# One-hots of an expert scatter moved from VectorE to GpSimd and ScalarE

## The reference

```python
u = U[ib]                                   # [tokens, 8 heads, 16 picks, 2048]
h = gelu(einsum('thkd,td->thk', u, xb))
w = gate * h
y = einsum('thk,thkd->td', w, V[ib])
```

## Time and profile before

| | |
|---|---|
| median of 3 runs | 3977.99 us (3966.75 to 3984.16) |
| profiled execution | 3977.78 us |
| its span | 3975.9 us |
| mean granted TensorE clock | 0.911 |
| busy: PE, DVE, POOL, ACT | 84%, 47%, 25%, 13% |
| units 9 to 15 of the U stage | 1789.4 to 2133.1 us |
| scatter of the second half | 2133.1 to 2200.4 us |
| V stage | 2200.4 to about 2755 us |

### The profile page before, as it was taken

How to read it: one execution, slowest core, us unless ns; L and a number is a source line. 1 busy time by engine, 2 the same in 40 slices (tenths; PEclk the granted TensorE clock), 3 DMA queues, 4 the chain that set the end, 5 groups by cost and what they waited for, 6 DMA issues and landing times. The chain is left out here.

```text
span 3975.9 us, 37603 instructions
## 1 busy us (share of the span) xinstructions
PE 3338.9 (84%) x15266; PEld 2682.0 (67%) x15266; DVE 1868.3 (47%) x3292; ACT 499.1 (13%) x835; POOL 998.5 (25%) x678
## 2 busy tenths in 40 slices
PE   7999999999989946300236999997999999999999
PEld 6878887888878835200134555553888788889888
DVE  3892102100000788998999544444244545555200
ACT  1002111100002100100013000001122122222100
POOL 0000000000000347877784454443000111112000
PEclk9999999999999977655557999998999999999999
DMA  4333332344364899999994899996333222221342
GB/s 167 141 135 138 139 120 81 128 157 150 130 234 155 303 387 371 377 348 357 366 335 154 289 337 332 348 332 248 117 117 117 106 85 85 79 81 64 138 151 103
DMA packets 164645, 795.35 MB, mean 200 GB/s; under 512 B 15064, under 2 KB 64728, under 8 KB 98920
## 3 DMA queue, kind: packets, MB, share of 16 engines
q1 hardware_dynamic: 106408, 419.61, 30.1%
q0 software_dynamic: 58064, 373.33, 25.2%
HBM read 790.78 MB, written 2.10 MB: 199 GB/s over the span
## 5 line engine op out<-in xcount | busy, mean ns | idle before, releaser
L351 PE MATMUL PS<-mem,ring 128*128 128x256 f32 (+1 forms) x4608 | 1035.2, 387 | 0.0
L351 PEld LDWEIGHTS PS<-mem,ring 128*128 128x128 f32 x4608 | 880.4, 191 | 152.4 <-issue 4.6
L957 POOL DMA_INDIRECT mem<-in_peer_u,idx x256 | 566.1, 2211 | 390.9 <-DVE mem L1398 155.3
L1690 PE MATMUL PS<-mem,ring 128*128 128x256 f32 x2816 | 640.3, 383 | 9.9 <-DVE ring L2078 9.9
L1398 DVE CUSTOM_DVE_ANT_0 mem<-mem 128x2048 f32<-128x2048 f32 x256 | 584.4, 2283 | 40.8 <-DMA mem<-in_peer_u,idx 40.1
L1690 PEld LDWEIGHTS PS<-mem,ring 128*128 128x128 f32 x2816 | 530.4, 192 | 84.5 <-issue 16.3
L1421 DVE SCALAR_TENSOR_TENSOR mem<-mem 128x768 f32<-128x768 f32 x256 | 260.9, 1019 | 294.8 <-DMA mem<-in_peer_vg,idx 287.6
L1123 PE MATMUL PS<-mem 128*128 128x128 f32 x512 | 132.7, 394 | 306.9 <-DVE mem L1386 305.5
L968 POOL DMA_INDIRECT mem<-in_peer_vg,idx x256 | 282.3, 1103 | 341.3 <-DVE mem L1421 298.6
L1123 PEld LDWEIGHTS PS<-mem 128*128 128x128 f32 x512 | 99.5, 255 | 340.4 <-DVE mem L1386 262.8
L1666 POOL TENSOR_TENSOR mem<-mem,ring 128x512 f32<-128x512 f32 x84 | 111.2, 1342 | 787.2 <-DVE mem L2183 575.0
(11 more groups left out here) (338 smaller groups left out, 2810.2 us busy)
## 6 DMA issues: line engine op xcount, KB each, us to landing
ring<-in_first_tiles SPq DMA_DIRECT2D x144, 1024.0 KB
ring<-in_dn_tiles SPq DMA_DIRECT2D x88, 1024.0 KB, 4.9
mem<-in_peer_vd SPq DMA_DIRECT2D x128, 640.0 KB
ring<-in_out_panels SPq DMA_DIRECT2D x16, 2048.0 KB, 8.8
ring<-in_w_out SPq DMA_DIRECT2D x8, 2048.0 KB, 12.5
ring<-in_peer_wq SPq DMA_DIRECT2D x8, 2048.0 KB, 8.7
ring<-in_mem_w_kv SPq DMA_DIRECT2D x8, 2048.0 KB, 34.0
mem<-in_peer_u,idx POOLq DMA_INDIRECT x256, 7.5
```

The lines of the kernel that those rows point to most:

```text
L351: last = nc.tensor.matmul(PS[:, 4 + n % 4, 0:T if wide else TX], wslot[:, slot_of[n], k, :], x, start=(k == 0), stop=(k == KT - 1))
L957: nc.gpsimd.indirect_dma_start(Ug[:, at % US, :], None, a["peer_u"][0], bass.IndirectOffsetOnAxis(ap=idx[:, n, j:j + 1], axis=0)).then_inc ...
L1690: ins = nc.tensor.matmul(bank_of(n), wts[:, n % WS, k, :], hT[:, k, :], start=(k == 0), stop=(k == KT - 1))
```

## The change

The one-hots no longer come from DVE alone. In the first half POOL makes `first`, each behind a gather, and ACT makes `second` in two activations, Abs(i2 - iota) and Relu(1 - that). They are spread over units 9 to 15 (112 steps, 128 tokens). In the second half DVE makes `first`, and POOL makes `second`, behind the first four V gathers. ACT's `gates` of a unit move behind its one-hots, and `picks_evict(0)` to unit 8. PE waits for two semaphores in place of one.

```diff
-        FIRST_HOT = 12
+        FIRST_HOT = PH + 1
+        STEPS = (HN - FIRST_HOT) * PTOP
+        def hot_tokens(at):
+            s = at - FIRST_HOT * PTOP
+            return range(s * P // STEPS, (s + 1) * P // STEPS) if s >= 0 else range(0)
...
                                 bass.IndirectOffsetOnAxis(ap=idx[:, n, j:j + 1], axis=0)).then_inc(u_in[at % US], 16)
+                            for t in hot_tokens(at):
+                                pool.wait_ge(it_out, 1)
+                                if t >= OS:
+                                    pool.wait_ge(oh_used, t - OS + 1)
+                                nc.gpsimd.tensor_scalar(first[:, t % OS, :], iota[:, :], turned[:, 0, t:t + 1],
+                                                        turned[:, 2, t:t + 1], ALU.is_equal, ALU.mult).then_inc(hot_pool, 1)
...
+                            if at == GS:
+                                for t in range(P, MT * P):
+                                    pool.wait_ge(it_out, MT)
+                                    pool.wait_ge(oh_used, t - OS + 1)
+                                    nc.gpsimd.tensor_scalar(second[:, t % OS, :], iota[:, :], turned[:, 1, t - P:t - P + 1],
+                                                            None, ALU.is_equal).then_inc(hot_pool, 1)
...
-                            pe.wait_ge(oh_ready, n + 1)
+                            pe.wait_ge(hot_pool, n + 1)
+                            if m == 0:
+                                pe.wait_ge(hot_act, n + 1)
+                            else:
+                                pe.wait_ge(hot_dve, t + 1)
...
-                            act.wait_ge(oh_ready, P * m)
+                            act.wait_ge(hot_pool, P)
+                            act.wait_ge(hot_act, P)
...
+                    def second_hot(t):
+                        act.wait_ge(it_out, 1)
+                        if t >= OS:
+                            act.wait_ge(oh_used, t - OS + 1)
+                        nc.scalar.activation(second[:, t % OS, :], iota[:, :], ACT.Abs, bias=turned[:, 1, t:t + 1],
+                                             scale=-1.0).then_inc(hot_abs, 1)
+                        act.wait_ge(hot_abs, t + 1)
+                        nc.scalar.activation(second[:, t % OS, :], second[:, t % OS, :], ACT.Relu, bias=1.0,
+                                             scale=-1.0).then_inc(hot_act, 1)
...
-                        for later in beside.get(n, ()):
-                            gates(later)
-                            done += 1
...
-                        if n == FIRST_HOT - 2:
+                        if n == PH:
                             picks_evict(0)
-                        if n >= FIRST_HOT:
-                            for g in range(8 * (n - FIRST_HOT), 8 * (n - FIRST_HOT) + 8):
-                                w_evict(g)
+                        for j in range(PTOP):
+                            for t in hot_tokens(n * PTOP + j):
+                                second_hot(t)
+                                if t % 4 == 3 and t > 3:
+                                    w_evict(t // 4 - 1)
+                        for later in beside.get(n, ()):
+                            gates(later)
+                            done += 1
                         gelu(n)
...
-                    def one_hots(n):
+                    def first_hot(n):
...
-                        nc.vector.tensor_scalar(second[:, n % OS, :], iota[:, :], turned[:, 1, t:t + 1], None, ALU.is_equal)
                         nc.vector.tensor_scalar(first[:, n % OS, :], iota[:, :], turned[:, 0, t:t + 1], turned[:, 2, t:t + 1],
-                                                ALU.is_equal, ALU.mult).then_inc(oh_ready, 1)
+                                                ALU.is_equal, ALU.mult).then_inc(hot_dve, 1)
...
-                            if n >= FIRST_HOT:
-                                for t in range(2):
-                                    one_hots(2 * (at - FIRST_HOT * PTOP) + t)
```

More of the change, by code:

```diff
@@ L903, in build @@
              m_scale, m_scaled, mt_done, mt_out, h_sum, h_roots, h_scale, xn_done, q_out, sc_done, sc_out, chain, max_ready,
-             exp_ready, found, den_ready, u_used, gelu_ready, w_ready, kk_taken, kv_taken, it_done, it_out, oh_ready, oh_used, w_done,
+             exp_ready, found, den_ready, u_used, gelu_ready, w_ready, kk_taken, kv_taken, it_done, it_out, hot_pool, hot_abs, hot_act,
+             hot_dve, oh_used, w_done,
              w_out, vd_used, vg_used, y_dense, y_added, f_squares, f_roots, f_scale, y_ready, f_chain, xn2_ready, nt_done,
@@ L910, in build @@
                 "found", "den_ready", "u_used", "gelu_ready", "weights_ready", "kk_taken", "kv_taken", "picks_transposed",
-                "picks_out", "onehot_ready", "onehot_used", "scatter_done", "scatter_out", "vd_used", "vg_used", "y_dense",
+                "picks_out", "onehot_pool", "onehot_distance", "onehot_act", "onehot_dve", "onehot_used", "scatter_done",
+                "scatter_out", "vd_used", "vg_used", "y_dense",
                 "y_added", "f_squares", "f_roots", "f_scale", "y_ready", "f_chain", "xn2_ready", "xn2_transposed", "hT_out", "pool_step",
@@ L1261, in _ @@
                     picks_evict(1)
-                    for g in range(P // 4, MT * P // 4):
+                    for g in range(P // 4 - 1, MT * P // 4):
                         w_evict(g)
@@ L1382, in one_hots @@
                             dve.wait_ge(it_out, m + 1)
-                        if n >= OS:
-                            dve.wait_ge(oh_used, n - OS + 1)
-                        nc.vector.tensor_scalar(second[:, n % OS, :], iota[:, :], turned[:, 1, t:t + 1], None, ALU.is_equal)
+                        dve.wait_ge(oh_used, n - OS + 1)
                         nc.vector.tensor_scalar(first[:, n % OS, :], iota[:, :], turned[:, 0, t:t + 1], turned[:, 2, t:t + 1],
-                                                ALU.is_equal, ALU.mult).then_inc(oh_ready, 1)
+                                                ALU.is_equal, ALU.mult).then_inc(hot_dve, 1)
                     for n in range(2):
@@ L1411, in _ @@
                     for n in range(P, MT * P):
-                        one_hots(n)
+                        first_hot(n)
                     for n in range(HN):
```

## The result

The changed kernel takes 4083.76 us (median of 4 runs) against 3981.07 us for the kernel before in the same session: ratio 1.0258, 95% interval 1.0237 to 1.028. The profiled execution has a span of 4082.3 us, 106.4 us more than before.

A forecast was written before the change was run, and what follows sets the result against it. The prediction took DVE to bound heads 12 to 15, with POOL gathers let in only between products. It summed 3978 + 21 (first half) + 5 (second half) = 4004 us, with a range of 3945 to 4068.

The forecast's parts named there:

- What bounds the kernel; losses reach the end whole: Heads 9 to 15 and second-half scatter: DVE bounds heads 12 to 15; the V stage waits, so losses reach the end.
- A gather is let in only between products: POOL instructions reading SBUF enter only between two-input DVE instructions; gathers end about 0.81 us behind a product, 0.94 us free.
- I take 0.3 us: First half: assumed length of one POOL one-hot, taken from a POOL select of 0.29 us.
- So the gather waits for a whole further product: Heads 9 to 15: four-buffer loop grows from 9.96 to 12.85 us, 3.21 us a step, +21 us with late rows.
- DVE's gain, at most 40 us: Heads 12 to 15: without one-hots on DVE, steps fall from 3.12 to 2.49 us at best, 40 us gained.
- ACT costs nothing: First half: `second` as two activations makes ACT 1.7 us a step where 3.1 are there, so no cost.
- Rival 4: First half: ACT reloads its table for Abs and Relu, 1.28 us a load, over +140 us; chance 0.02.
- Second half, +5 us from 0.49 us a token: Second-half scatter: a token goes from 0.45 to 0.49 us with DVE and POOL partly overlapping, +5 us.
- My upper bound of 0.63 a token: Second half: DVE and POOL one-hots strictly in turn, 0.29 + 0.34 us a token, a loss of 23 us.
- Rival 1: First half: the gather slips in right behind the one-hot, 2.65 us a step, about 3955 us; chance 0.18.
- Rival 2: First half: half the steps slip in, some 2.93 us a step, about 3979 us, no change; chance 0.22.
- Rival 3: First half: two products lost for a gather, 3.8 us a step, +92, about 4070 us; chance 0.18.

The follow-up runs named there:

- run 7: Kernel before the change, with DVE's product replaced by a one-input sum over the same buffer: 3960.31 us, ratio 0.995.
- run 8: Changed kernel with DVE's product replaced by a one-input sum over the same buffer: 3945.52 us, ratio 0.9924.
- run 5: Changed kernel with three memsets in place of each POOL one-hot of the first half: 3980.44 us, ratio 1.0004.
- run 6: Changed kernel with POOL's first-half one-hot made over 32 of its 128 columns: 4044.48 us, ratio 1.0184.
- run 3: Changed kernel without POOL one-hots: first half `first` on DVE, `second` on ACT; second half as before the change: 3953.55 us, ratio 0.9934.
- run 4: Changed kernel with both first-half one-hots on ACT, second half as before the change: 3958.08 us, ratio 0.9947.
- run 12: Kernel with only the second half changed, its POOL one-hot made over 32 of 128 columns: 3972.42 us, ratio 0.9979.
- run 11: The kernel of run 3 measured once more, on the chip of run 10: 3955.53 us, ratio 0.9931.
- run 10: The kernel of run 3, but ACT makes `first` for every second token of the first half: 3957.58 us, ratio 0.9937.
- run 9: Changed kernel with POOL's one-hots in groups behind every fourth gather instead of behind each: 4082.87 us, ratio 1.0248.

## Why the prediction was off

The direction and the place were right: slower, in heads 9 to 15, with gathers and one-hots held to the ends of products. The size was not: +26 us forecast, 103 measured, above the range, which ended at 4068. The first half is off by 73 us (365 forecast, 437.9 measured), the second by 10.

1. *What bounds the kernel; losses reach the end whole.* Right: +94.2 and +14.7 us, less 4.7 us by which head 9 begins earlier in this execution, and a V stage that is 2.1 us longer, are the 106 us of span.
2. *A gather is let in only between products.* Right, and now shown by runs 7 and 8 and not only read off: with a DVE sum of one SBUF input the same gathers take 0.94 us. The Trainium skill's rule (SBUF — State Buffer, Who interferes with whom) names just this pair, a two-input VectorE instruction and a GpSimd instruction that reads; run 5, where POOL only writes, agrees at 0.22 us for the longest memset. The gather behaves like such a reader.
3. *"I take 0.3 us" for a POOL one-hot.* A mis-sized term. Unhindered it takes 0.78 to 0.82 us. The select of the earlier trace rows is another instruction; that it has the same size says little. What stood as the upper end, 0.37 us, was half of an add and no bound at all. Run 6 prices the term: 0.32 us of length are 36 of the 94 us. By the same line the whole 0.48 us would be 54 (an estimate), but only because each one-hot pays for it, which the sum of point 4 doesn't have.
4. *"So the gather waits for a whole further product", a loop of 12.85 us, 3.21 us a step.* The step that failed. The sum charged the exclusion as a delay in the loop of four buffers: one product and 0.6 us in every four steps. But the pattern that it describes, one-hot and gather both held, would need the ends of two products in every step, and a step has one. POOL's own time was never added up.

   The trace shows that POOL's queue sets the pace, and not the buffers. In heads 12 to 15 POOL is in an instruction for 234 of 248 us, and a gather starts 5.9 us (median) after the end of the product that freed its buffer, where it was 1.1 us before. A step is what POOL has to do in it: a gather of 1.0 us, 1.14 one-hots of 0.80 and 0.2 of gaps, 2.1 us together, and 1.77 us of being held by the step's one product. That is 3.9 us; 3.87 were measured. The hold is taken from the same trace, so this first agreement is bookkeeping. The check is run 6, where the hold comes out the same: with its shorter one-hot the sum gives 3.5, and 3.51 were measured.

   In this sum the one-hot's length is paid on each of the 128; in the forecast's loop it is paid once in four steps. With the measured length (0.67 us behind the product's end in place of 0.15) that loop would be 13.35 us, 3.34 a step, and heads 9 to 15 would come out at +35 us (an estimate by its own sum), not at +94.
5. *DVE's gain, at most 40 us.* Its place was right: without POOL, runs 3 and 4 get 26 to 28 us in heads 9 to 15. The 2.49 us a step of head 11 did not come about over 64 steps: with the DMA share at 0.98 to 0.99 they took 2.68 and 2.75. This bound is not in the prediction's sum.
6. *ACT costs nothing.* Right: Abs 0.40 and Relu 0.31 us, no table load more than before (76), and runs 3 and 4 are faster with it. Rival 4 fell.
7. *Second half, +5 us from 0.49 us a token.* The sign was right, +14.7 us was measured. The term again is POOL's length, 0.59 us with one scalar for the 0.29 assumed. My upper bound of 0.63 a token came near the measured 0.58 to 0.62 for the wrong reason, by luck: it added strict turns between DVE and POOL to a POOL length that was half the real one, and run 12 shows that no turns are needed to explain it.
8. *Rivals.* Rivals 1 and 2 fell. Rival 3 gave the step (3.8 us for 3.87) and was nearest in time (about 4070), with a chance of 0.18, and the range had been cut at its middle. Its picture, one-hot and gather each missing a gap, is seen in head 13 but not as a rule: 27 of 72 one-hots were held. That it came so near with a one-hot of 0.3 us is in part luck.

The best kernel of the study is run 3 (and again run 11): `second` on ACT, `first` on DVE, POOL left to its gathers, 0.7% faster than before. Runs 4 and 10 lie within its interval.

## What to carry to other kernels

In this kernel each DVE product with two SBUF inputs held one POOL instruction that reads, for 1.77 us on average, and further ones got in while DVE stood idle, or in the first 0.04 us of a product. Before work is given to a POOL that also issues gathers, add up its own time for each DVE instruction: the lengths of its reading instructions, and one wait. If that is more than DVE's step, POOL is the bound. Here the reading instructions went from one to 2.14 a step, and POOL's 25% of busy time over the whole run told nothing of that: in heads 12 to 15 it was in a gather for 178 of 200 us already. And where a price rests on a row of another instruction, keep the range as wide as the doubt: the length was off by a factor of 2.7, and a case with nearly the measured time was on the list of rivals.

## What the runs showed of the hardware that was not expected

- POOL's tensor-scalar on float32 over 128 partitions: 0.78 us at the shortest for 128 columns with two scalars and 0.46 for 32 (3.3 ns a column); 0.59 and 0.35 with one scalar (2.5 ns a column). A memset of 128 columns takes 0.204, a select 0.29, DVE's version of the same one-hot 0.34.
- An indirect gather on POOL takes 2.8 us beside DVE's two-input product and 0.94 beside a one-input sum of the same length. In runs 3 and 8 the steps of heads 12 to 15 are nearly the same all the same (2.68 and 2.70 us): the DMA share is 0.99 in both, so the hold-up of the gathers costs little there.
- At the end of each of the 64 products of heads 12 to 15 exactly one POOL instruction was under way, in the changed kernel and in runs 6 and 9, in whatever order one-hots and gathers stood.
